# adaLN group 5 of a diffusion backbone's mLSTM layer: from TensorE's rows in the heads to VectorE during the projections

## The chip, the cores and the metric

The kernel runs on one core of one Trainium2 chip. The metric is the device time of one execution in microseconds; less is better. It has a median of 1303.7 us over three runs (1302.11 to 1309.29). All data are fp32.

## The reference, cut to what matters

One step of a backbone of four layers, on 128 context tokens and 256 latent tokens of width 1024. Every layer has a token mixer (pooling, mLSTM, latent attention, pooling) and then a mixture of 16 experts, 2 for each token. Ahead of both stands an RMS norm whose result is modulated by adaLN:

```
m = silu(cvec) @ w_ada[i] + b_ada[i]        # (1024) @ (1024, 6144): shift, scale, gate for mixer, then for experts
h = modulate(rmsnorm(x, norm_mix[i]), m0, m1);  x = x + m2 * mixer(h)
h = modulate(rmsnorm(x, norm_ffn[i]), m3, m4);  x = x + m5 * moe(h)
```

There are two conditioning vectors, one for context, one for latents. The mLSTM mixer of layer 1 computes

```
proj = h @ w_in                              # q, k: 4 heads x 128; v, o: 4 heads x 256; 16 gates
h_f, st_f = mlstm_chunkwise(q, k, v, g[0], g[1], init_f)     # forward scan
h_b, st_b = mlstm_chunkwise(flip of all, g[2], g[3], init_b) # backward scan
y = (sigmoid(o) * rmsnorm_per_head(h_f + flip(h_b)) * head_g) @ w_out
```

## The kernel before, in words

The six adaLN vectors of a layer are made in three groups of 2048 columns: group g belongs to layer g // 3, so groups 3, 4 and 5 are layer 1's. Group 5 holds the experts' scale and gate of layer 1, and groups 6 and 7 belong to layer 2. Each group needs 8 row blocks of `w_ada` (128 x 2048, 1 MB). There are two ways to make a group.

By TensorE: `ada(g, rows)` (L539) takes a block from the ring and runs four matmuls of 128x2 by 128x512 into four strips of PSUM bank 7. A matmul shows as two instructions, so a block is 8 and a group 64.

By VectorE: `mix(g, rows)` (L1644) multiplies a block by the conditioning value of each partition and adds it to an accumulator in SBUF, once for each of the two conditioning vectors (L1661; the first block is a plain product, L1664). The first block's part for accumulator 0 is made by ScalarE (`mixed_first`, L1295, L1300), and VectorE waits for it (`acc_set`). `ada_sum(g)` (L550) then sums both accumulators over the partitions by 8 matmuls (16 instructions).

Both ways go on alike: ScalarE copies bank 7 to `mrow` (`mod_rows`, L1288, L1293), TensorE turns it (`ada_columns`, L562, L566), VectorE adds the bias (`mod_columns`, L1624, L1629). Bank 7 and `mrow` hold one group at a time, so groups pass in order. Before, group 4 is mixed by VectorE and groups 5, 6 and 7 go by TensorE. The table `ACC` (L313) says where a group's accumulators lie, in pieces, since they live in space that is free at the time.

The ring (L53 to L56) has 12 slots of 1 MB for all weights. SP's queue loads the units in the order of the list `units`; unit u waits until unit u - 12 was used (L472).

TensorE's order in the mLSTM mixer (L701) is written out by hand: query and key projections (8 chunks), value projections (L729, 12 chunks of 128 tokens by 256 columns), the turns of the gate rows (L741), group 4's sum, gate projections (L750, 12 chunks), then the heads (L813). Projections use banks 5 and 6 in turn, and ScalarE copies each chunk out (L1358 for values, L1362 and L1364 for gates).

A head h makes its scores, the broadcast of running maxima (L782), two key products, and six numerators (L793), three for each direction, in three banks in turn. VectorE masks (L1775), weighs (L1787 to L1792), copies the two new states out of PSUM (L1805, L1806), divides (L1812 to L1820) and gates (L1827). ScalarE makes the exponentials (L1376, L1379), copies numerators (L1411), makes the carry's exponential (`carry_of`, L1386), the squares (L1420) and the output gate (L1429), and copies the turned head (L1394). VectorE's order for a head is: mask of head h+1, states of h, weights of h+1, division of direction 0, carry of h+1, division of direction 1, gating of h. The rows of groups 5, 6 and 7 stand between TensorE's instructions: for example four rows of group 5 while the first head's weights are made, two among the numerators of head 0, two behind the first numerator of head 1, and six of group 7 after the last head.

## Time and profile before

| What | Value |
|---|---|
| Median of three runs | 1303.7 us |
| The profiled execution's own time | 1300.99 us |
| Its span | 1299.3 us |
| Mean granted TensorE clock | 0.949 |
| TensorE busy | 1175.7 us, 90% |
| VectorE busy | 548.3 us, 42% |
| ScalarE busy | 328.3 us, 25% |
| Layer 1's value projections | from 316.2 us |
| Layer 1's gate projections | from 360.8 us |
| Heads | from 404.0 us |
| Output projection | from 478.2 us |

The span runs from the first to the last instruction of the profiled execution; its own time is what the run took as a whole. Busy times overlap between engines. A granted clock of 1.00 is 2.4 GHz, 0.50 is 1.2 GHz.

### The profile page before, as it was taken

Reading aid. Unit: us, or ns where it says so; the run is one execution under the profiler, and the core shown is the slowest. Engines: PE = TensorE matmul, PEld = TensorE weight load, DVE = VectorE, ACT = ScalarE, POOL = GpSimd, SP = SyncE. Lnnn points to the kernel's source line nnn. Section 1 sums busy time; section 2 is a strip of 40 time slices with the busy share of each in tenths; the row PEclk is TensorE's granted clock in tenths of the full one; section 3 lists DMA queues with packets and bytes.
Section 4 is the critical chain, followed back from the end, with each engine's and each line's share of the span. In section 5 each row is a group of like instructions: output and inputs, shape, how many; then the busy total and the mean of one; then the engine's idle time right before and its main releaser. Section 6 shows DMA issues by size and latency. Waiting matters only on the chain.

```text
span 1299.3 us, 24638 instructions
## 1 busy us (share of the span) xinstructions
PE 1175.7 (90%) x10246; PEld 702.6 (54%) x10246; DVE 548.3 (42%) x1318; ACT 328.3 (25%) x721; POOL 123.2 (9%) x188
## 2 busy tenths in 40 slices
PE   4788998889999989899987999999799997799986
PEld 2346554446886545655535844555564545564544
DVE  1355211259002549731117876459841115741113
ACT  1240111240123540411115411340411114411113
POOL 2000110210000000101120000000011120011111
PEclk9898998999999999899997999899799997799998
DMA  9999999799426789398979973106489987578983
GB/s 352 402 422 420 416 407 422 299 388 336 176 97 225 270 314 388 120 398 343 405 307 363 347 282 127 59 1 251 187 315 362 415 332 298 213 300 355 376 364 137
DMA packets 89708, 389.56 MB, mean 300 GB/s; under 512 B 10456, under 2 KB 38604, under 8 KB 53240
## 3 DMA queue, kind: packets, MB, share of 16 engines
q1 hardware_dynamic: 71568, 336.61, 65.7%
q0 software_dynamic: 17456, 51.07, 10.8%
q8 instruction: 85, 1.39, 0.4%
q10 hardware_dynamic: 568, 0.23, 0.1%
q14 instruction: 31, 0.25, 0.1%
HBM read 370.96 MB, written 27.96 MB: 307 GB/s over the span
## 4 chain that ended last, share of the span: by engine, by line
PE 75%; DMA 12%; DVE 5%; ACT 4%; issue 2%; POOL 1%; ACTq 0%; POOLq 0%; SPq 0%; DVEq 0%
PE bank L525 68%; DMA sb_ring<-in_w_ada 3%; PE bank L1068 3%; DMA sb_ring<-in_w_exp_down 2%; DMA slot_out<-sb_arena,sb_homes 2%; DMA sb_arena<-slot_out,sb_slots 2%; DMA token_rows<-sb_arena 1%; POOL sb_arena L2331 1%; DMA sb_arena<-in_b_ada 1%; PE bank L1086 1%; DVE sb_xT L2184 1%; DVE sb_hT L1671 1%; PE bank L1017 1%; DMA sb_arena<-token_rows,sb_rows 1%; ACT sb_hT L1340 1%
## 5 line engine op out<-in xcount | busy, mean ns | idle before, releaser
L525 PE MATMUL bank<-sb_ring,sb_arena 128*32 128x256 f32 (+1 forms) x6112 | 451.0, 429 | 19.3 <-DMA sb_ring<-in_w_exp_down 8.3
L525 PEld LDWEIGHTS bank<-sb_ring,sb_arena 128*32 128x32 f32 x6112 | 212.9, 111 | 199.2 <-issue 110.3
L525 PE MATMUL bank<-sb_ring,sb_hT 128*128 128x256 f32 x624 | 143.0, 392 | 4.1 <-ACT sb_hT L1330 4.1
L525 PE MATMUL bank<-sb_arena 128*128 128x128 f32 (+11 forms) x776 | 137.9, 355 | 8.7 <-ACT sb_arena L1497 2.3
L525 PEld LDWEIGHTS bank<-sb_ring,sb_hT 128*128 128x128 f32 x624 | 122.4, 197 | 25.5 <-issue 7.8
L2131 DVE TENSOR_TENSOR sb_arena<-sb_arena,bank 128x256 f32<-128x256 f32 x40 | 16.8, 421 | 251.8 <-PE bank L525 251.8
L525 PEld LDWEIGHTS bank<-sb_arena 128*128 128x128 f32 (+2 forms) x776 | 99.7, 188 | 42.1 <-issue 18.6
L1661 DVE SCALAR_TENSOR_TENSOR sb_arena<-sb_ring,sb_cond,sb_arena 128x2048 f32<-128x2048 f32 (+1 forms) x56 | 114.3, 2079 | 0.1
L525 PE MATMUL bank<-sb_arena,sb_ring 128*128 128x384 f32 (+2 forms) x288 | 93.9, 501 | 0.0
L525 PE MATMUL bank<-sb_hT,sb_ring 128*128 128x384 f32 x256 | 84.9, 494 | 2.6 <-ACT sb_hT L1330 2.6
L2138 DVE COPY sb_arena<-bank 128x512 f32<-128x512 f32 x40 | 27.7, 692 | 131.8 <-PE bank L525 131.8
L525 PEld LDWEIGHTS bank<-sb_arena,sb_ring 128*128 128x128 f32 (+1 forms) x288 | 49.1, 178 | 41.3 <-issue 15.9
L525 PEld LDWEIGHTS bank<-sb_hT,sb_ring 128*128 128x128 f32 x256 | 49.2, 193 | 37.5 <-issue 4.3
L1518 ACT ACTIVATE sb_arena<-bank 128x512 f32<-128x512 f32 x40 | 23.9, 597 | 158.8 <-PE bank L1068 141.1
L525 PE MATMUL bank<-sb_ring,sb_cond 128*2 128x512 f32 x448 | 55.6, 621 | 6.7 <-DMA sb_ring<-in_w_ada 6.4
L1310 ACT ACTIVATE sb_scratch<-sb_xT 128x768 f32<-128x768 f32 (+1 forms) x45 | 31.4, 713 | 108.8 <-DVE sb_xT L1688 98.9
L1522 ACT ACTIVATE sb_arena<-bank 128x256 f32<-128x256 f32 x40 | 15.4, 385 | 155.4 <-PE bank L525 155.4
L1671 DVE SCALAR_TENSOR_TENSOR sb_hT<-sb_xT,sb_amp,sb_rstd 128x128 f32<-128x128 f32 (+1 forms) x128 | 43.1, 411 | 15.4 <-ACT sb_rstd L1323 15.4
L2310 POOL DMA_INDIRECT slot_out<-sb_arena,sb_homes x27 | 27.1, 1004 | 223.1 <-DVE sb_arena L2138 219.9
L2299 POOL DMA_INDIRECT sb_arena<-token_rows,sb_rows x36 | 36.8, 1021 | 119.9 <-DVE sb_slots L2166 71.6
L1534 ACT ACTIVATE sb_arena<-bank 128x512 f32<-128x512 f32 x40 | 23.9, 597 | 82.5 <-PE bank L525 82.5
L2290 POOL DMA_DIRECT2D token_rows<-sb_arena x12 | 6.5, 540 | 389.0 <-ACT sb_arena L1497 388.9
(343 smaller groups left out, 1162.8 us busy)
## 6 DMA issues: line engine op xcount, KB each, us to landing
sb_ring<-in_w_ada SPq DMA_DIRECT2D x96, 1024.0 KB, 10.7
sb_ring<-in_w_exp_gate SPq DMA_DIRECT2D x60, 1024.0 KB, 10.1
sb_ring<-in_w_exp_up SPq DMA_DIRECT2D x60, 1024.0 KB, 12.7
sb_ring<-in_w_exp_down SPq DMA_DIRECT2D x60, 1024.0 KB, 15.0
sb_ring<-in_w_mlstm_in SPq DMA_DIRECT2D x12, 1024.0 KB, 9.4
token_rows<-sb_arena POOLq DMA_DIRECT2D x12, 512.0 KB, 4.2
slot_out<-sb_arena POOLq DMA_DIRECT2D x9, 512.0 KB, 8.9
sb_scratch<-in_w_exp_gate SPq DMA_DIRECT2D x4, 1024.0 KB, 7.1
```

Of the source, the lines that this page charges most:

```text
L525: return pe.matmul(out, lhsT, rhs, start=first, stop=last)
L1068: ins = pe.transpose(ps[2 + c][:, k * P:(k + 1) * P], xg[:, (o - 1) % 2, (4 * c + k) * P:(4 * c + k + 1) * P], ident[:, :])
L1310: act.activation(sq[:, a:b, :], xT[:, a:b, :], ACT.Square).then_inc(sq_ready, 1)
L1518: act.activation(xgT[:, o % 2, 0:4, :].rearrange("p k s -> p (k s)"), ps[2][:, :], ACT.Copy).then_inc(xa_ready, 1)
L1522: act.activation(sil[:, :], ps[0][:, 0:FE], ACT.Silu).then_inc(sil_ready, 1)
L1534: act.activation(ysb[:, o % 2, 0:512], ps[5][:, :], ACT.Copy).then_inc(ya_ready, 1)
L1661: ins = v.scalar_tensor_tensor(out=ap, in0=w[:, a:b], scalar=cond[:, k, c:c + 1], in1=ap, op0=ALU.mult, op1=ALU.add)
L1671: v.scalar_tensor_tensor(out=hT[:, k, a:b], in0=xT[:, k, a:b], scalar=gain[:, k, c:c + 1], in1=rstd[:, a:b], op0=ALU.mult, op1=ALU.mult).t ...
L2131: v.tensor_tensor(hid[:, :].rearrange("p (j q) -> p j q", j=2), sil[:, :].rearrange("p (q j) -> p j q", j=2), ps[1][:, 0:FE].rearrange("p ...
L2138: v.tensor_copy(ysb[:, o % 2, 512:1024], ps[6][:, :]).then_inc(yb_ready, 1)
L2299: g.indirect_dma_start(out=xg[:, (o - 1) % 2, :], out_offset=None, in_=Xg, in_offset=bass.IndirectOffsetOnAxis(ap=rows[:, o:o + 1], axis=0 ...
L2310: g.indirect_dma_start(out=Yg, out_offset=bass.IndirectOffsetOnAxis(ap=homes[:, o:o + 1], axis=0), in_=ysb[:, o % 2, :], in_offset=None, b ...
```

## The change: group 5 by VectorE, turns and group 4's sum earlier

Group 5 gets accumulators. Accumulator 0 lies in three pieces of 1024, 512 and 512 columns, accumulator 1 in one of 2048; they take the place of the gate rows (`grow`), which are last read by the turns and by two small DMAs (`out_m`), and of parts of `scratch` that the output gate of heads 2 and 3 is written to later. Its eight blocks are loaded between the value weights and behind the first gate weights. The turns move ahead of the value projections, group 4's sum behind value chunk 3 and its columns behind chunk 6. Group 5's sum comes behind gate chunk 2 and its columns behind chunk 5. In the heads the rows of groups 6 and 7 are placed anew, and `mod_rows` of group 6 moves from among head 1's numerators to behind them. Heads are computed in the order 0 to 3, as before.

```diff
+        in_gates = [[(view(8204, 1024), 0, 1024), (scratch[:, 512:1024], 1024, 1536), (scratch[:, 1536:2048], 1536, 2048)],
+                    [(view(6156, 2048), 0, 2048)]]
-        ACC = {4: in_squares, 8: in_values, 9: in_keys, 10: in_latents, 11: in_keys}
+        ACC = {4: in_squares, 5: in_gates, 8: in_values, 9: in_keys, 10: in_latents, 11: in_keys}
-        ADA_MIXER = [(), (5, 6, 7), (), ()]
+        ADA_MIXER = [(), (6, 7), (), ()]
...
# order of loads
                     if i == 0:
                         mixed_units(4, 6, 7)
+                    else:
+                        mixed_units(5, 2 * i - 2, 2 * i - 1)
                 for i in range(4):
                     add((w[:, 2048 + i * 256:2048 + (i + 1) * 256], KC, 256), 2048, (o_full, NT * (i + 1)))
+                    if i == 0:
+                        mixed_units(5, 6, 7)
...
# TensorE: the turns now stand ahead of the value projections; in these
-                ada_sum(4)
+                        if c == 3:
+                            ada_sum(4)
+                        if c == 6:
+                            ada_columns(4)
# and in the gate projections
-                        if c == 4:
-                            ada_columns(4)
+                        if c == 2:
+                            ada_sum(5)
+                        if c == 5:
+                            ada_columns(5)
# heads
-                ada(g4, 0, 1, 2, 3)
+                ada(near, 0, 1, 2, 3)
...
+                    if h == 2:
+                        ada_columns(near)
                     for c in range(2 * NT):
                         numerator(h, c // NT, c % NT)
-                        if h % 2 == 0 and c == (2 if h == 0 else 3):
-                            ada(g4 + h // 2, 4, 5)
-                        if h % 2 and c == 0:
-                            ada(g4 + h // 2, 6, 7)
-                        if h % 2 and c == 4:
-                            ada_columns(g4 + h // 2)
-                        if h % 2 and c == 5:
-                            ada(g5 + h // 2, 0, 1)
-                        if h == 2 and c == 0:
-                            ada(g5, 2, 3)
+                        if h == 1 and c == 2:
+                            ada(near, 6, 7)
+                        if h == 2 and c == 3:
+                            ada(far_group, 0, 1)
+                    if h == 0:
+                        ada(near, 4, 5)
+                    if h == 2:
+                        ada(far_group, 2, 3)
                     if h:
                         turn_head(h - 1)
-                ada(g6, 2, 3, 4, 5, 6, 7)
+                ada(far_group, 4, 5, 6, 7)
...
# ScalarE: value chunks, gate chunks, heads
+                    if c == 4:
+                        mod_rows(4)
+                        mixed_first(5)
-                    if c == 1:
-                        mod_rows(4)
+                    if c == 3:
+                        mod_rows(5)
-                        if h % 2 and c == NT - 1:
-                            mod_rows(ADA_MIXER[1][h // 2])
+                    if h == 1:
+                        mod_rows(ADA_MIXER[1][0])
                     if h + 1 < MH:
                         carry_of(h + 1)
...
# VectorE, after group 4 and the copy of the turned rows
+                v.wait_ge(out_m, 32)
+                mix(5, 0, 1, 2)
                 mod_columns(4)
+                mix(5, 3, 4, 5, 6, 7)
+                mod_columns(5)
```

Here `near` is group 6 and `far_group` group 7. VectorE adds group 6's bias in head 2.

## Rows read from the trace of the kernel before

**Rows 1.** The page: the chain that ended last, by engine.
```profile
PE 75%; DMA 12%; DVE 5%; ACT 4%; issue 2%; POOL 1%; ACTq 0%; POOLq 0%; SPq 0%; DVEq 0%
```
**Rows 2.** Stretches: length; PE, PEld, DVE, ACT, POOL busy (instructions); clock, DMA share, GB/s.
```profile
316.00:358.00 42.00, 42.00 (x198) 36.63 (x196) 8.87 (x6) 4.85 (x13) 0.00 (x0) 1.00 0.57 210
361.00:403.00 42.00, 41.95 (x196) 36.59 (x195) 0.19 (x1) 9.31 (x24) 0.00 (x0) 1.00 0.25 85
441.00:455.00 14.00, 14.00 (x82) 8.12 (x81) 7.12 (x23) 8.88 (x30) 1.07 (x2) 1.00 0.91 355
```
**Rows 3.** TensorE in order of time, projections: start, us, instructions, [idle before].
```profile
316.24 41.60 PE L525 MATMUL bank<-sb_ring,sb_hT 128*128 128x256 f32 x192
357.77 1.28 PE L746 MATMUL bank<-sb_ident,sb_arena 4*128 4x4 f32 x18
358.98 1.46 PE L525 MATMUL bank<-sb_scratch,sb_order 128*2 128x512 f32 x10
...
360.81 17.53 PE L525 MATMUL bank<-sb_ring,sb_hT 128*128 128x256 f32 x80
378.18 0.60 PE L566 MATMUL bank<-sb_ident,sb_mrow 128*128 128x128 f32 x4
378.62 24.34 PE L525 MATMUL bank<-sb_ring,sb_hT 128*128 128x256 f32 x112
403.99 1.38 PE L525 MATMUL bank<-sb_arena 128*128 128x128 f32 x10 [1.03 <-ACT sb_arena L1369]
```
**Rows 4.** VectorE in order of time: group 4, and head 3's last division.
```profile
302.71 1.28 DVE L1661 SCALAR_TENSOR_TENSOR sb_arena<-sb_ring,sb_cond,sb_arena 128x1024 f32<-128x1024 f32 x1
...
307.37 1.28 DVE L1661 SCALAR_TENSOR_TENSOR sb_arena<-sb_ring,sb_cond,sb_arena 128x1024 f32<-128x1024 f32 x1
...
322.53 2.35 DVE L1661 SCALAR_TENSOR_TENSOR sb_scratch<-sb_ring,sb_cond,sb_scratch 128x2048 f32<-128x2048 f32 x1
...
469.78 1.28 DVE L1820 SCALAR_TENSOR_TENSOR sb_arena<-sb_arena 128x256 f32<-128x256 f32 x3
```
**Rows 5.** ScalarE in order of time: first block, mrow, head 1's last numerator, squares.
```profile
282.70 1.99 ACT L1300 ACTIVATE sb_scratch<-sb_ring,sb_cond 128x2048 f32<-128x2048 f32 x1
...
368.76 0.58 ACT L1293 ACTIVATE sb_mrow<-bank 128x512 f32<-128x512 f32 x1
...
438.26 0.39 ACT L1411 ACTIVATE sb_arena<-bank 128x257 f32<-128x257 f32 x1 [0.92 <-PE bank L525]
...
471.93 0.41 ACT L1420 ACTIVATE sb_arena<-sb_arena 128x256 f32<-128x256 f32 x1
```
**Rows 6.** The chain that ended last: heads' last numerators and the return to TensorE.
```profile
422.58 0.39 ACT sb_arena L1411
...
431.07 5.85 PE bank L525 x18
...
453.93 0.39 ACT sb_arena L1411
```
**Rows 7.** TensorE in order of time, heads, columns as in rows 3.
```profile
417.84 1.90 PE L525 MATMUL bank<-sb_ring,sb_cond 128*2 128x512 f32 x16
...
431.07 0.70 PE L525 MATMUL bank<-sb_arena,sb_hT 128*128 128x257 f32 x2 [2.49 <-DVE sb_arena L1806]
...
461.49 0.70 PE L525 MATMUL bank<-sb_arena,sb_hT 128*128 128x257 f32 x2 [2.92 <-DVE sb_arena L1806]
...
476.58 0.82 PE L810 MATMUL bank<-sb_ident,sb_arena 128*128 128x128 f32 x6
478.22 0.95 PE L525 MATMUL bank<-sb_w_rt,sb_mod 128*1 128x16 f32 x32 [0.81 <-ACT sb_arena L1394]
```
**Rows 8.** Stretches of 2 us behind the gap at 431.07, columns as in rows 2.
```profile
431.00:433.00 2.00, 1.93 (x7) 1.65 (x8) 1.76 (x7) 2.00 (x8) 1.07 (x2) 0.77 0.98 414
433.00:435.00 2.00, 2.00 (x7) 1.54 (x6) 0.59 (x2) 0.31 (x2) 0.00 (x0) 0.50 0.98 397
435.00:437.00 2.00, 2.00 (x11) 1.70 (x10) 1.39 (x6) 1.08 (x4) 0.00 (x0) 0.87 0.06 25
```

More of the change, by code:

```diff
@@ L727, in mlstm @@
                         ins.then_inc(qk_full, 1)
+                pe.wait_ge(rows_done, 1)
+                for d in range(2):
+                    for q, src in enumerate((rA, rS, rE)):
+                        for t in range(NT):
+                            c = ((d * 3 + q) * NT + t) * MH
+                            ins = pe.transpose(ps[4][:, 64 + c:64 + c + MH], src[:, d, t * P:(t + 1) * P], ident[0:MH, 0:MH])
+                ins.then_inc(turns_full, 1)
                 for i in range(4):
@@ L739, in mlstm @@
                         ins.then_inc(v_full, 1)
-                pe.wait_ge(rows_done, 1)
-                for d in range(2):
-                    for q, src in enumerate((rA, rS, rE)):
-                        for t in range(NT):
-                            c = ((d * 3 + q) * NT + t) * MH
-                            ins = pe.transpose(ps[4][:, 64 + c:64 + c + MH], src[:, d, t * P:(t + 1) * P], ident[0:MH, 0:MH])
-                ins.then_inc(turns_full, 1)
-                ada_sum(4)
+                        if c == 3:
+                            ada_sum(4)
+                        if c == 6:
+                            ada_columns(4)
                 for i in range(4):
@@ L765, in mlstm @@
                 pe.wait_ge(l_ready, 12)
-                g4, g5, g6 = ADA_MIXER[1]
+                near, far_group = ADA_MIXER[1]
                 state["item"] = 0
@@ L845, in mlstm @@
                 project(r, lambda k: (qT if k % 2 == 0 else kT)[:, k // 2, :], hsT_ready, [8] * KC)
-                ada_columns(g6)
+                ada_columns(far_group)
             def mla(r):
@@ L1430, in mlstm @@
                 turned_head(MH - 1)
-                mod_rows(ADA_MIXER[1][2])
+                mod_rows(ADA_MIXER[1][1])
                 mixed_first(8)
@@ L1838, in mlstm @@
                     divided(h, 0)
-                    if h % 2:
-                        mod_columns(ADA_MIXER[1][h // 2])
+                    if h == 2:
+                        mod_columns(ADA_MIXER[1][0])
                     if h + 1 < MH:
@@ L2240, in _ @@
                 if kind == 1:
-                    mod_columns(ADA_MIXER[1][2])
+                    mod_columns(ADA_MIXER[1][1])
                 if L == 0:
```

## The prediction

> **What bounds the kernel now.** I read the page first. The chain that ended last is TensorE for 75% of the span [rows 1], so the question at each edit is whether it lies on TensorE's own line or beside it. Then a table of stretches over layer 1's mLSTM, then each engine's order of instructions there, and last the chain of waits through the four heads.
>
> The stage has two parts with different limits. In the value and gate projections (316 to 403 us) TensorE is busy without a break, VectorE works 8.9 us of the first 42 and 0.2 of the second 42 [rows 2]: TensorE bounds, and whatever it is given there lengthens the stage one for one. In the heads (404 to 478 us) it is mixed: TensorE is full from 441 to 455 [rows 2], but stands idle for 2.49 us before 431.07 and for 2.92 before 461.49, both times for VectorE's copy of a state, L1806 [rows 7]. The chain says why [rows 6]: from the evacuation of a head's last numerator (422.58) it runs in the code's order through ScalarE's carry (L1386), VectorE's division (L1820), ScalarE's squares and exponential (L1420, L1429), VectorE's mask (L1775) and state copy, and only at 431.07 back to TensorE: 8.5 us in which TensorE has nothing of its own but turns, scores, keys and the next head's first numerator. The adaLN rows stand in that gap as filling. For the last pair (453.93 to 461.49) it is 7.56 us [rows 6, 7], since no mask follows.
>
> **The change part by part.** Times are those of the profiled execution before; "heads frame" means that the shift of the projections is added at the end.
>
> *Turns and group 4's sum.* They took 357.77 to 358.98 and 358.98 to 360.81 between the projections [rows 3], 1.21 and 1.83 us on TensorE. Now they stand before the first and after the fourth value chunk. Both are moved along a line without gaps: 0. What they wait for is there: VectorE's last row of group 4 ends at 322.53 + 2.35 = 324.9 [rows 4], the sum comes at 316.24 + 1.21 + 4 x 3.46 = 331.3 (a chunk is 41.5/12 = 3.46, from 316.24 to 357.77). Value projections then end at 317.45 + 41.5 + 1.83 + 0.44 (group 4's columns, 378.18 to 378.62) = 361.2.
>
> *Group 5 on VectorE.* A row of group 4 costs 307.37 - 302.71 = 4.66 us, from one operation of 2048 and two of 1024 [rows 4]. That gives 1.04 ns a column and 0.13 us an operation. Group 5 has 2048, 1024 and twice 512: 2.26 + 1.20 + 2 x 0.66 = 4.78 us. VectorE begins at 325.1 (after copying rowc), does row 0's half (a plain product; 1.3 by estimate, 2.35 at most, without effect on what follows) and row 1's half (2.3), and stops at 328.7: its other half starts from what ScalarE sets (acc_set). ScalarE gets there after value chunk 4 (ends 336.6; copy 0.4), mod_rows(4) (0.58) and three pieces of the 2048 that took 1.99 [rows 5]: 339.8. This wait is free for VectorE, which has nothing else; behind ScalarE's 2.7 us stands only the copy of chunk 5 (full at 340.0). Then row 1's rest 2.5, row 2 4.8, mod_columns(4) 0.35 (its columns are turned at 343.9), rows 3 to 7 23.9: **371.4**.
>
> *Group 5's sum and columns.* They come after the third and sixth gate chunk. Chunk 2 ends at 361.2 + 3 x 3.46 = **371.6**, so TensorE arrives 0.2 us after VectorE is done. Gate chunks 3 to 11 and all heads queue behind this wait. The sum costs 1.83 and the columns 0.44, both on a line without gaps. The lower bound of the wait is 0; the upper takes the full durations 2.35 + 1.28 + 2 x 0.75 a row, 5.1, so 0.35 more over nearly 7 rows: 2.4 late, 2.2 us of wait. I take 0, since group 4's spacing was measured in the same loop. Gate projections end at 371.6 + 1.83 + 9 x 3.46 + 0.44 = 404.9, against 402.7 before: **+2.2 us**, 1.83 of it the sum and 0.44 the columns that leave the heads.
>
> The Trainium skill, VectorE: DVE Perf Modes, section "The TRN2 errata — SBUF-src ops pay a fixed extra latency per instruction", speaks against cutting an operand into pieces: each instruction pays a fixed cost, and it gives (N+151)/0.96 ns for an fp32 operation of two tensors, 0.69 us at 512 and 2.29 at 2048. The rows agree that there is such a part, but the spacing shows it smaller. An estimate from the page's formula is 4.89 us a row; VectorE would end some 0.8 us later, and the sum would be 0.6 us longer.
>
> *Loads.* On SP's queue group 5's eight rows move ahead of v2, v3 and the gate weights, to where rows of group 4 free slots. Queue and bytes stay the same, nothing is issued twice. The last value and first gate weights then wait for slots that come free with the last key chunk (316) and the third value chunk (328), in a stretch where DMA is 25% to 57% busy [rows 2]; they are wanted from 350 and 361 on. The latest, o2 and o3, wait for group 5's row 1 (342) and are wanted after 382: 0. Below zero is excluded, as TensorE waits for no load here.
>
> *The heads.* 64 instructions leave; 16 of this form (128x512, two rows as at 417.84 [rows 7]) take 1.83 us start to start, as the sum of group 4 does [rows 3]: 7.3 us of TensorE, and one set of columns. What is that worth? I follow the order head by head.
> Head 0: its two rows stood between numerators 2 and 3, on the chain. They now follow the last numerator, in the gap: -1.83. The return to TensorE for head 1 is at 431.07 - 1.83 = 429.24; TensorE is empty from 426.7, 2.5 us, as long as before (2.49).
> Head 1: two rows of group 6 go from the gap in front to the numerators, behind number 2: +1.83; the columns are gone: -0.44. Last numerator evacuated at 437.8, before 438.26 [rows 5]. But mod_rows(6) now stands between this evacuation and the carry, 0.55 us of ScalarE on the chain: +0.55. The return for head 2 is then 437.8 + 0.55 + 8.4 = 446.8, what it was (446.83). In front of it TensorE had four rows, 3.7 us, that are gone: it is empty from 442.8, 4.0 us, where it had no gap.
> Head 2: same numerators, same two rows among them. After the gaps of 2.49 and 2.92 us [rows 7] the granted clock was 0.50 for 0.92 + 2.00 + 0.52 = 3.4 us (0.77, 0.50 and 0.87 in three stretches of 2 us [rows 8]), which on a full TensorE costs half of it, 1.7 us. A gap of 4.0 should do the same here: **+1.7**. The lower bound is 0, the upper two such stretches, 3.4.
> Head 3: return at 455.6 + 7.56 = 463.2, before 461.49; the clock falls as before. Without columns (-0.44) the last evacuation is 1.2 late, at 469.9. Turning head 2 no longer waits for two rows, so ScalarE's squares, which began at 471.93 though VectorE had divided by 469.78 + 1.28 = 471.06 [rows 4, 5], are not pushed back by it: -0.87. Four last rows instead of six end at 474.2, and the last turn waits for the gated head at 476.0, where it used to wait for the rows until 476.58 [rows 7]. The output projection starts at 477.65 instead of 478.22: **-0.6 us**.
> So of 7.7 us taken out only 0.6 arrive (2.3 but for the clock). What is late next is the ScalarE and VectorE chain, not TensorE.
> Two short gaps in front of the output projection (1.8 and 0.8 us, before 0.8) may bring one more half-clock stretch, 0 to 1.7; I take 0, as the gap of 1.03 at 403.99 [rows 3] brought none.
>
> *Later.* Loads of the output weights come earlier, since rows of group 6 free slots sooner; TensorE waits for none of them now, so 0. From the output projection on the order is the same, group 7's columns still follow the projection, and routing and experts start from it: the shift is carried through.
>
> **Sum:** +2.2 - 0.6 = +1.6 us. The profiled execution took 1300.99 us (span 1299.3), so it would take 1302.6; the median of the runs is 2.7 us above it, so 1305.3. Range of this case alone: 1302 to 1309.
>
> **Rivals.**
> (a) TensorE bounds the heads after all. For it: 90% busy over the span, and no idle from 441 to 455 [rows 2]. Against it: three idle stretches on the chain. Then the whole 7.3 + 0.44 comes off: +2.2 - 7.7 = -5.5, 1298.2.
> (b) The gap before head 2 doesn't lower the clock, or the one before head 1 no longer does. For it: the clock is full in all of 441 to 455 today. Against: both gaps over 2.4 us were followed by it. +1.6 - 1.7 = 0, 1303.6; with both -1.8.
> (c) TensorE waits at group 5's sum, because VectorE's rows take their full durations or ScalarE's part comes late; the shift to VectorE then isn't a hidden one. Decides when a row exceeds 4.8 us. +1.6 + 2.2 = +3.8, 1307.5.
> (d) The other side, slower by over 0.5%: TensorE's clock. The filling was what kept the gaps short. If each of the three gaps between heads brings two stretches at half clock and the output projection starts in one, it is 3 x 1.7 + 1.7 = 6.8 on top, +8.4, 1312.1. Place: numerators behind each gap. It decides once a gap is followed by more than one stretch of 3.4 us; the 2.49 and 2.92 were not.
>
> **How the numbers follow.** About 0.5% (6.5 us) is what a measurement of this kernel can tell from no change; its three runs spread over 7 us. Forecast 0.52, (a) 0.14, (b) 0.16, (c) 0.10, (d) 0.08. The range 1298.5 to 1311 takes in (b), (c), nearly all of (a), and leaves (d) and stray runs out. Faster by over 0.5%: a part of (a) with the spread, 0.08. Slower: (d) and the upper spread of (c) and the forecast, 0.13. Same: 0.79.
>
> **What would show it.** Right: TensorE without a gap in both projections, the gate projections ending 2.2 us later after the turns; VectorE's last group 5 operation within 1 us of gate chunk 2; the heads' stretch within 1.5 us of 74.2; a new gap of about 4 us before head 2's second numerator with clock 0.50 behind it; group 6's mrow copy just ahead of the carry. Wrong: heads shorter by over 4 us (then (a)), a TensorE wait on VectorE L1661 over 1 us (then (c)), or a difference that lies outside 316 to 521 us, which would mean that a load or the clock elsewhere decides.

## The result, and the profile after

The changed kernel takes 1307.11 us (median of 18 runs, 1302.97 to 1315.81) beside 1302.51 us for the kernel before on the same chip: a ratio of 1.0046, 95% interval 1.0026 to 1.0065. Run a second time beside other kernels (e11 below) it had 1.0084 (1.0051 to 1.0118). So it is slower, by 0.3 to 1.2%, where the forecast was +1.6 us, 0.12%. The measured 1307.11 lies in the range that was given (1298.5 to 1311) and the sign is that of the sum, but the sum was too small: +4.6 us in the medians, +6.2 between the two profiled executions (1307.2 and 1300.99). That the time still lies in the range is due to the range, which is 12.5 us wide, and not to the sum.

The profiled execution after has a span of 1305.2 us and a mean granted clock of 0.946. In its code the lines stand a little lower: L525 is now L531 (TensorE's products), L1661 is L1675 (VectorE's mixing), L1806 is L1824 (state copy), L1411 is L1425, L1386 is L1400, L1293 is L1304. In the experiments they are off by a few lines more or less; L1822, L1826, L1808 and L1804 are all the state copy.

TensorE's order of time in the projections, after (columns as in [rows 3]):

```profile
318.07 1.28 PE L740 MATMUL bank<-sb_ident,sb_arena 4*128 4x4 f32 x18
319.28 14.08 PE L531 MATMUL bank<-sb_ring,sb_hT 128*128 128x256 f32 x64
333.29 1.46 PE L531 MATMUL bank<-sb_scratch,sb_order 128*2 128x512 f32 x10
...
346.02 27.79 PE L531 MATMUL bank<-sb_ring,sb_hT 128*128 128x256 f32 x128
373.74 0.60 PE L531 MATMUL bank<-sb_arena,sb_order 128*2 128x512 f32 x2
...
375.57 10.63 PE L531 MATMUL bank<-sb_ring,sb_hT 128*128 128x256 f32 x48
...
408.39 1.38 PE L531 MATMUL bank<-sb_arena 128*128 128x128 f32 x10 [1.03 <-ACT sb_arena L1383]
```

There is no idle time from the turns (318.07) to the end of the gate projections; the stretch to the first scores is 90.32 us, and was 316.24 to 403.99, 87.75 us [rows 3]. Group 5's sum starts at 373.74 without a wait. VectorE was done just in time:

```profile
342.03 1.28 DVE L1675 SCALAR_TENSOR_TENSOR sb_arena<-sb_ring,sb_cond,sb_arena 128x1024 f32<-128x1024 f32 x1 [11.64 <-ACT sb_scratch L1311]
343.23 1.41 DVE L1675 SCALAR_TENSOR_TENSOR sb_scratch<-sb_ring,sb_cond,sb_scratch 128x512 f32<-128x512 f32 x2
...
367.38 1.41 DVE L1675 SCALAR_TENSOR_TENSOR sb_scratch<-sb_ring,sb_cond,sb_scratch 128x512 f32<-128x512 f32 x2
368.70 3.54 DVE L1675 SCALAR_TENSOR_TENSOR sb_arena<-sb_ring,sb_cond,sb_arena 128x2048 f32<-128x2048 f32 x2
372.16 1.41 DVE L1675 SCALAR_TENSOR_TENSOR sb_scratch<-sb_ring,sb_cond,sb_scratch 128x512 f32<-128x512 f32 x2
```

A row takes 372.16 - 367.38 = 4.78 us, and the last one ends at 373.57, 0.17 us ahead of the sum. VectorE's 11.64 us wait for ScalarE (342.03) cost TensorE nothing.

The heads are where the forecast and the trace part. TensorE's order of time after (columns as in [rows 7]):

```profile
411.53 5.02 PE L531 MATMUL bank<-sb_ring,sb_cond 128*2 128x512 f32 x32
...
421.37 0.70 PE L531 MATMUL bank<-sb_arena,sb_hT 128*128 128x257 f32 x2 [0.41 <-DVE sb_arena L1824]
...
434.92 1.22 PE L531 MATMUL bank<-sb_arena,sb_hT 128*128 128x257 f32 x2 [2.29 <-DVE sb_arena L1824]
...
452.65 1.22 PE L531 MATMUL bank<-sb_arena,sb_hT 128*128 128x257 f32 x2 [3.64 <-DVE sb_arena L1824]
...
459.57 1.90 PE L531 MATMUL bank<-sb_ring,sb_cond 128*2 128x512 f32 x16 [1.42 <-issue]
...
471.44 0.70 PE L531 MATMUL bank<-sb_arena,sb_hT 128*128 128x257 f32 x2 [3.45 <-DVE sb_arena L1824]
...
484.33 0.88 PE L821 MATMUL bank<-sb_ident,sb_arena 128*128 128x128 f32 x6 [1.77 <-DVE sb_arena L1845]
486.02 1.01 PE L531 MATMUL bank<-sb_w_rt,sb_mod 128*1 128x16 f32 x32 [0.81 <-ACT sb_arena L1408]
```

And four lines of the kernel before that the table below needs beside those of [rows 7]:

```profile
406.89 3.62 PE L525 MATMUL bank<-sb_ring,sb_cond 128*2 128x512 f32 x32
...
415.48 0.70 PE L525 MATMUL bank<-sb_arena,sb_hT 128*128 128x257 f32 x2 [0.42 <-DVE sb_arena L1806]
...
446.83 0.70 PE L525 MATMUL bank<-sb_arena,sb_hT 128*128 128x257 f32 x2
...
449.62 1.90 PE L525 MATMUL bank<-sb_ring,sb_cond 128*2 128x512 f32 x16
```

The number in brackets is TensorE's idle time and who ended it. Before there were two gaps over 2 us [rows 7]; now there are three (2.29, 3.64, 3.45), a new one of 1.42 among head 2's numerators, and 1.77 behind the last head. The heads take 77.63 us instead of 74.23. A head's "return" is the moment when TensorE goes on behind the head's first numerator, with the state that VectorE copied (415.48, 431.07, 446.83 and 461.49 before). From one return to the next:

| Stretch | Before | After | Difference | Forecast |
|---|---|---|---|---|
| Turns or value projections to first scores | 87.75 | 90.32 | +2.6 | +2.2 |
| First scores to return in head 0 | 11.49 | 12.98 | +1.5 | 0 |
| to return in head 1 | 15.59 | 13.55 | -2.0 | -1.8 |
| to return in head 2 | 15.76 | 17.73 | +2.0 | +1.8 |
| to return in head 3 | 14.66 | 18.79 | +4.1 | +1.7 |
| to the output projection | 16.73 | 14.58 | -2.2 | -2.3 |
| Output projection, to group 7's columns | 42.26 | 43.57 | +1.3 | 0 |

That is +7.3 us for the whole, of which the forecast had +1.6. Outside these stretches, where the order of instructions is the same, the two executions differ by +1.8 us ahead of 316 us and by -3.2 behind the output projection. Both are differences of single executions: the start of the first row of the table lies anywhere from 314.7 to 318.1 us in the thirteen profiles of this document (316.75 in the changed kernel's second one), and behind the output projection the clock was at 1.2 GHz for 94.5 us before and 87.6 us after, which is worth 3.4 us where TensorE is busy. The medians say +4.6.

The granted clock in stretches of 2 us, behind the gaps at 452.65 and 486.02 (columns as in [rows 2]; the clock is the third number from the right):

```profile
451.00:453.00 2.00, 0.35 (x1) 0.35 (x2) 1.99 (x7) 1.23 (x5) 0.11 (x1) 0.74 0.00 0
453.00:455.00 2.00, 2.00 (x6) 1.54 (x6) 1.77 (x5) 1.64 (x7) 0.96 (x2) 0.50 0.37 131
455.00:457.00 2.00, 2.00 (x6) 1.63 (x5) 0.18 (x1) 0.15 (x1) 0.00 (x0) 0.50 0.00 0
457.00:459.00 2.00, 1.15 (x3) 0.34 (x1) 1.14 (x6) 0.77 (x2) 0.00 (x0) 0.55 0.00 0
...
487.00:489.00 2.00, 2.00 (x5) 1.13 (x4) 1.78 (x4) 1.35 (x1) 0.00 (x0) 0.50 0.99 406
```

Around the gap of 3.64 us the clock is at 1.2 GHz for 1.04 + 2 + 2 + 1.8 = 6.8 us, twice as long as behind the 2.49 before [rows 8]. It begins at 451.96, 0.7 us before TensorE returns, and ends in the wait at 458.8, so some of it falls on idle time and costs nothing.

The wait that the forecast did not have is seen on VectorE, after:

```profile
457.75 0.16 DVE L1830 SCALAR_TENSOR_TENSOR sb_arena<-sb_arena 128x3 f32<-128x3 f32 x1 [2.57 <-ACT sb_arena L1425]
...
458.36 0.88 DVE L1836 TENSOR_SCALAR sb_arena<-sb_arena 128x256 f32<-128x256 f32 x3
459.28 0.19 DVE L1643 TENSOR_TENSOR sb_mod<-bank,sb_b_ada 128x32 f32<-128x32 f32 x1
```

L1643 is `mod_columns(6)`. It was moved to head 2 behind the division of direction 0, and this division starts only when numerator 2 of head 2 is copied. TensorE's first row of group 7 (`ada(7, 0)`, behind numerator 3 of head 2) needs bank 7 free, and so waits for it: it ends at 459.28 + 0.19 = 459.47 on VectorE, and the row starts at 459.57 on TensorE. The same 0.10 us lie between the two in e2 (453.91 and 454.01) and e11 (459.62 and 459.72). Numerators 4 and 5 and head 3's keys stand behind it.

And ScalarE, after, with `mod_rows(6)` on the chain between the last numerator's copy and the carry:

```profile
443.67 0.39 ACT L1425 ACTIVATE sb_arena<-bank 128x257 f32<-128x257 f32 x1 [0.48 <-PE bank L531]
443.95 0.59 ACT L1304 ACTIVATE sb_mrow<-bank 128x512 f32<-128x512 f32 x1
444.43 0.84 ACT L1400 ACTIVATE sb_arena<-bank,sb_m_all 128x256 f32<-128x256 f32 x2
```

### The profile page after: what moved, and what is told of

Its sections match the earlier page's. It is cut to its first block, busy times and chain, and to the rows that moved or that the text cites. A ratio compares the mean times of both kernels' runs of the same rounds, so it can differ in the third digit from the quotient of the medians.

```text
span 1305.2 us, 24581 instructions
## 1 busy us (share of the span) xinstructions
PE 1178.1 (90%) x10198; PEld 716.1 (55%) x10198; DVE 582.3 (45%) x1347; ACT 330.6 (25%) x724; POOL 123.2 (9%) x188
## 4 chain that ended last, share of the span: by engine, by line
PE 74%; DMA 11%; DVE 6%; ACT 4%; issue 3%; POOL 1%; SPq 1%; ACTq 0%; POOLq 0%; DVEq 0%
PE bank L531 68%; DMA sb_ring<-in_w_ada 3%; PE bank L1079 3%; DMA slot_out<-sb_arena,sb_homes 2%; DMA sb_ring<-in_w_exp_down 2%; DMA sb_arena<-slot_out,sb_slots 2%; POOL sb_arena L2349 1%; DMA sb_arena<-in_b_ada 1%; DVE sb_xT L2202 1%; PE bank L1097 1%; DVE sb_hT L1685 1%; PE bank L1028 1%; DMA sb_arena<-token_rows,sb_rows 1%; DMA slot_out<-sb_arena 1%; ACT sb_hT L1351 1%
## 5 line engine op out<-in xcount | busy, mean ns | idle before, releaser
L531 PE MATMUL bank<-sb_ring,sb_arena 128*32 128x256 f32 (+1 forms) x6112 | 456.9, 430 | 21.7 <-DMA sb_ring<-in_w_exp_down 9.7
L531 PEld LDWEIGHTS bank<-sb_ring,sb_arena 128*32 128x32 f32 x6112 | 228.0, 111 | 192.3 <-issue 114.1
L531 PE MATMUL bank<-sb_arena 128*128 128x128 f32 (+11 forms) x776 | 140.1, 359 | 8.2 <-ACT sb_arena L1511 2.3
L1675 DVE SCALAR_TENSOR_TENSOR sb_arena<-sb_ring,sb_cond,sb_arena 128x2048 f32<-128x2048 f32 (+1 forms) x70 | 139.2, 2025 | 11.9 <-ACT sb_scratch L1311 11.6
L531 PE MATMUL bank<-sb_ring,sb_hT 128*128 128x256 f32 x624 | 140.6, 387 | 4.2 <-ACT sb_hT L1341 4.2
L531 PEld LDWEIGHTS bank<-sb_ring,sb_hT 128*128 128x128 f32 x624 | 119.9, 194 | 25.0 <-issue 8.2
L531 PEld LDWEIGHTS bank<-sb_arena 128*128 128x128 f32 (+2 forms) x776 | 100.8, 190 | 42.4 <-issue 20.1
L531 PE MATMUL bank<-sb_arena,sb_ring 128*128 128x384 f32 (+2 forms) x288 | 95.2, 506 | 0.0
L531 PE MATMUL bank<-sb_hT,sb_ring 128*128 128x384 f32 x256 | 87.1, 503 | 2.6 <-ACT sb_hT L1341 2.6
L531 PEld LDWEIGHTS bank<-sb_arena,sb_ring 128*128 128x128 f32 (+1 forms) x288 | 49.7, 180 | 42.0 <-issue 17.0
L531 PEld LDWEIGHTS bank<-sb_hT,sb_ring 128*128 128x128 f32 x256 | 50.5, 198 | 38.7 <-issue 6.0
L531 PE MATMUL bank<-sb_ring,sb_cond 128*2 128x512 f32 x384 | 50.2, 650 | 8.9 <-DMA sb_ring<-in_w_ada 7.2
```

Of the source, the lines that this page charges most:

```text
L531: return pe.matmul(out, lhsT, rhs, start=first, stop=last)
L1675: ins = v.scalar_tensor_tensor(out=ap, in0=w[:, a:b], scalar=cond[:, k, c:c + 1], in1=ap, op0=ALU.mult, op1=ALU.add)
```

## The experiments

Theory after the result: the heads are bound by a chain through ScalarE and VectorE, so rows taken from TensorE there earn nothing unless they stood on the chain; they leave gaps, and gaps bring TensorE's half clock; and the new places put one wait on the chain. Rivals: TensorE bounds the heads; the half-clock stretches come by chance; the moves in the projections are what costs.

All ratios are to the kernel before on the same chip, from 6 to 18 runs of each kernel and 18 to 35 of the kernel before. The stretches are of each kernel's one profiled execution, and that of the kernel before is from the first chip only.

| Kernel | Ratio (95%) | Projections | Heads | Mean clock in heads | Output projection |
|---|---|---|---|---|---|
| before | 1 | 87.75 | 74.23 | 0.95 | 42.26 |
| changed | 1.0046 (1.0026, 1.0065) | 90.32 | 77.63 | 0.89 | 43.57 |
| changed again (e11) | 1.0084 (1.0051, 1.0118) | 90.32 | 80.36 | 0.85 | 43.71 |
| e1 rows behind head 2 | 1.0005 (0.9981, 1.0029) | 90.32 | 77.36 | 0.85 | 43.75 |
| e2 changed, gaps filled | 0.9993 (0.9966, 1.0021) | 90.32 | 73.81 | 0.95 | 43.66 |
| e3 rows in the gaps | 0.9965 (0.9941, 0.9990) | 90.32 | 68.33 | 0.92 | 44.84 |
| e4 moves only | 1.0022 (0.9993, 1.0051) | 87.86 | 75.92 | 0.93 | 42.27 |
| e5 e3 filled | 0.9982 (0.9957, 1.0008) | 90.32 | 71.07 | 0.98 | 42.27 |
| e6 old places | 1.0005 (0.9979, 1.0032) | 90.32 | 74.02 | 0.88 | 42.26 |
| e7 before, gaps filled | 0.9961 (0.9929, 0.9993) | 87.76 | 72.50 | 0.98 | 42.27 |
| e8 two rows last | 0.9972 (0.9944, 1.0000) | 90.32 | 71.31 | 0.88 | 43.46 |
| e9 all by TensorE, in gaps | 0.9957 (0.9927, 0.9987) | 87.75 | 68.24 | 0.97 | 42.26 |
| e10 e5, sized | 0.9971 (0.9940, 1.0003) | 90.32 | 67.88 | 0.95 | 42.27 |

### e1: without the wait in head 2

```diff
-                        if h == 2 and c == 3:
-                            ada(far_group, 0, 1)
                     if h == 2:
-                        ada(far_group, 2, 3)
+                        ada(far_group, 0, 1, 2, 3)
```

> The changed kernel, with group 7's first two rows moved from behind numerator 3 of head 2 to behind its last numerator. Theory (wait): ada(7, 0) waits for VectorE's mod_columns(6), which stands behind VectorE's division of head 2, and TensorE's idle 1.42 us ahead of these rows lies on the chain. Then head 2's stretch (18.8 us between returns) shrinks by 1.4 for the wait and 1.8 for the rows, 3.2 in all, and the idle gap in front of head 3 shrinks from 3.45 to 1.6 us: the kernel is 3 us faster than the changed one, +1.5 to +3 us against the one before. Rival (TensorE bounds): the rows cost the same wherever they stand, so only the 1.4 us can come off. Rival (half clock): the second 3.4 us stretch of half clock in head 2 came from the wait; it goes too, 1.7 us more.

The wait is gone (no idle time but the returns), and the stretch from head 2's return to head 3's is 453.89 to 469.85, 15.96 us instead of 18.79: -2.8 where 3.2 were expected, and 1.8 of the 2.8 are the two rows' own time, which left the chain with the wait. The gap did not shrink to 1.6, though:

```profile
460.67 3.61 PE L531 MATMUL bank<-sb_ring,sb_cond 128*2 128x512 f32 x32
464.21 0.87 PE L821 MATMUL bank<-sb_ident,sb_arena 128*128 128x128 f32 x6
...
469.85 0.70 PE L531 MATMUL bank<-sb_arena,sb_hT 128*128 128x257 f32 x2 [3.25 <-DVE sb_arena L1822]
```

ScalarE in the same execution says why:

```profile
464.80 1.05 ACT L1406 ACTIVATE sb_arena<-bank,sb_vecs 128x384 f32<-128x384 f32 x2 [2.91 <-PE bank L821]
465.74 0.41 ACT L1432 ACTIVATE sb_arena<-sb_arena 128x256 f32<-128x256 f32 x1
```

ScalarE copies the turned head 1 (L1406) ahead of head 2's squares (L1432), and the turn (L821) now stands behind four rows. It comes at 464.21, and the squares start only at 465.74. In the changed kernel the last numerator's copy and the squares are 467.31 - 463.87 = 3.4 us apart, here 465.74 - 460.78 = 5.0. So four rows ahead of a turn were too many here. The whole heads took 77.36 us, with more half clock (mean 0.85). The ratio is below the changed kernel's 1.0046, but their intervals touch.

### e2: work added in the gaps

```diff
+                    for _ in range((0, 5, 8, 8)[h] if d == 0 and t == 0 else 0):
+                        mm(b, a[:, d, t * P:(t + 1) * P], vx[:, t, h, :], True, True)
                     ins = mm(b, a[:, d, t * P:(t + 1) * P], vx[:, t, h, :], True, t == 0)
```

> The changed kernel, with work added: the first product of the first numerator is repeated 5 times in head 1 and 8 times in heads 2 and 3 (same operands, same bank, result overwritten by the same), 21 x 0.43 = 9 us of TensorE, put where it is idle for 2.3, 3.6 and 3.45 us. Theory (clock): the half-clock stretches behind these gaps are caused by them. Filled gaps bring no stretch: -1.7 us for head 1, -1.7 to -3.4 for head 2, -1.7 for head 3, so 4 to 6 us faster than the changed kernel although it does more. Rival (the stretches come by chance or from something else): no faster, 0 to 1 us slower. Rival (TensorE bounds the heads): 9 us slower.

With 9 us of useless products TensorE is full across the gaps, and the heads take 73.81 us instead of 77.63, at a mean clock of 0.95 instead of 0.89. Only two idle times are left between head 0 and the last turn:

```profile
449.31 0.70 PE L531 MATMUL bank<-sb_arena,sb_hT 128*128 128x257 f32 x2 [0.20 <-DVE sb_arena L1826]
...
454.01 1.90 PE L531 MATMUL bank<-sb_ring,sb_cond 128*2 128x512 f32 x16 [1.84 <-issue]
```

The second is the wait for `mod_columns(6)` again, by itself: here, with the clock full around it, it is 1.84 us. From the return to this first row of group 7 it takes 454.01 - 449.31 = 4.70 us here, 449.62 - 446.83 = 2.79 in the kernel before and 459.57 - 452.65 = 6.92 in the changed one. So the wait is worth 1.9 us, and the half clock of the changed kernel the other 2.2. The ratio, 0.9993 (0.9966 to 1.0021), lies clear of the changed kernel's 1.0046 (1.0026 to 1.0065). "TensorE bounds the heads" would have made them 9 us longer and falls with this run. "By chance" is weakened, as three stretches went at once; e7 and e11 add to that.

### e3: the rows of groups 6 and 7 in the gaps

The calls that place these rows and columns in the changed kernel are taken out (not printed), and these put in:

```diff
                     for c in range(2 * NT):
                         numerator(h, c // NT, c % NT)
+                        if h == 1 and c == 0:
+                            ada(near, 6, 7)
+                        if h == 1 and c == 4:
+                            ada_columns(near)
+                        if h > 1 and c == 0:
+                            ada(far_group, 4 * h - 6, 4 * h - 5)
...
                     if h == 0:
                         ada(near, 4, 5)
+                    if h == 1:
+                        ada(far_group, 0, 1)
+                    if h == 2:
+                        ada(far_group, 4, 5)
```

with `mod_rows(6)` after head 1's numerator 2 and `mod_columns(6)` in head 1.

> The changed kernel with the rows of groups 6 and 7 placed in the gaps between heads and none among numerators: 4, 5 of group 6 behind head 0 and 6, 7 behind the first numerator of head 1; 0, 1 of group 7 behind head 1, 2, 3 behind head 2's first numerator, 4, 5 behind head 2, 6, 7 behind head 3's first numerator; none behind head 3. Group 6's copy to mrow stands after head 1's numerator 2, its columns after numerator 4. Theory (ScalarE and VectorE chain plus gaps): against the changed kernel -1.8 and -0.55 in head 1, -1.4 and -1.8 in head 2, and 2 to 4 half-clock stretches of 1.7 us less: 8 to 11 us faster than the changed one, so 3 to 6 us faster than the one before. Rival (TensorE bounds): the same rows at other places, at most 1.4 us faster than the changed one.

The heads take 68.33 us, 9.3 less than in the changed kernel with the same 16 blocks of rows, and the kernel is faster than the one before (0.9965). The rows cost nothing that shows in the gaps. What is left is the gap behind the last head:

```profile
474.08 1.54 PE L821 MATMUL bank<-sb_ident,sb_arena 128*128 128x128 f32 x6 [5.41 <-DVE sb_arena L1846]
476.30 1.01 PE L531 MATMUL bank<-sb_w_rt,sb_mod 128*1 128x16 f32 x32 [0.67 <-ACT sb_arena L1409]
```

The six turns take 1.54 us instead of 0.8 and the output projection 44.84 instead of 42.26: the half clock begins within the 5.41 idle us and lasts 10.2.

### e4: the moves in the value projections alone

The kernel before, with turns and group 4's sum and columns at their new places, and group 5 by TensorE as before.

> The kernel before with one part of the change alone: turns ahead of the value projections, group 4's sum behind value chunk 3, its columns behind chunk 6; group 5 stays with TensorE in the heads. Theory: 0 (within 1 us), as these are moves along a TensorE without gaps. Rival: the moves themselves cost the extra 2.6 us that the projections show, or ScalarE's copy to mrow among value chunks holds up TensorE; then 2 to 3 us slower.

Projections 87.86 us beside 87.75: the moves cost 0.1 us, and the 2.5 us up to 90.32 come with group 5's sum and columns (1.83 and 0.44). The ratio 1.0022 (0.9993 to 1.0051) doesn't tell it from no change. Its heads have the order of before and took 75.92, with one half-clock stretch more (clock 0.93), so 1.7 us of difference between two profiles can be the clock alone.

### e5 and e10: the last gaps filled with nothing

The edit is on top of e3's.

```diff
+                    for _ in range((0, 1, 0, 3)[h] if d == 0 and t == 0 else 0):
+                        mm(b, a[:, d, t * P:(t + 1) * P], vx[:, t, h, :], True, True)
...
                 pe.transpose(ps[2][0:8, 0:P], nout, ident[:, :]).then_inc(turns_full, 1)
+                for _ in range(16):          # 7 in e10
+                    mm(ps[3][:, 0:TOK], ident[:, :], xT[:, 0, :], True, True)
```

> The kernel with rows in the gaps (e3), plus work that computes nothing new: the first product of the first numerator repeated once in head 1 and three times in head 3, and 16 products of 128x128 by 128x384 into a free PSUM bank behind the last head's columns of n. They fill the idle 0.47, 1.63 and 5.41 us that e3 still has. Theory (clock): e3's 10.2 us at half clock from 472.3 on, behind its gap of 5.41 us, cost some 4 to 5 us of turns and output projection; filled, they go: 3 to 5 us faster than e3, 1293 to 1295 us beside 1301 for the kernel before. Rival (stretches come from something else): same as e3, or up to 0.5 us slower.

> As e5, with 7 products behind the last head instead of 16. In e5 they took 10.3 us, twice what was meant, and the last head's turn stood 4.9 us late behind them; the clock had no stretch there. Theory (chain): heads 66 to 67 us beside 71.1, output projection at full clock, 4 to 5 us faster than e5, so 7 to 8 faster than before. Rival: the 7 leave a gap that brings a half-clock stretch, 2 to 3 us faster than e5 only.

e5 was a miss in its size: 16 products are 32 instructions of 0.32 us, and the last turn stood behind them until 475.00:

```profile
464.68 10.49 PE L531 MATMUL bank<-sb_xT,sb_ident 128*128 128x384 f32 x32
475.00 0.82 PE L823 MATMUL bank<-sb_ident,sb_arena 128*128 128x128 f32 x6
```

In e10, with 14 instructions, the gap ahead of that turn is short:

```profile
467.10 4.68 PE L531 MATMUL bank<-sb_xT,sb_ident 128*128 128x384 f32 x14
472.68 0.87 PE L823 MATMUL bank<-sb_ident,sb_arena 128*128 128x128 f32 x6 [0.90 <-DVE sb_arena L1850]
```

In both the output projection runs at full clock, 42.27 us, where e3 had 44.84. Heads are 71.07 and 67.88 us. In the profiles the half clock behaves as expected. The medians fall short of what was expected: e5 is not faster than e3, and e10 is 4.1 us faster than the kernel before (1292.84 and 1296.92), not 7 to 8. 0.9982 and 0.9971 are not told apart from each other or from e3.

### e6: group 5's rows gone, the others at their old places

> The changed kernel, but in the heads groups 6 and 7 stand where they stood before: group 5's rows and columns are simply gone (none while the first weights are made, none in head 0, none behind head 1's first numerator). It separates the removal from the new places. Theory: -1.8 us (head 0's two rows) and -0.4 (columns), all else bound by the ScalarE and VectorE chain, so the heads take 72 us but for the clock; the emptied gaps (3.7 us at the start, 4.4 in front of head 1's second numerator, 2.9 in front of head 3's) each bring a half-clock stretch or two. Heads 72 to 76 us, beside 77.6 in the changed kernel, as neither the 1.4 us wait nor the rows among head 1's numerators are there: 0 to 4 us slower than before, 2 to 5 faster than the changed one. Rival (TensorE bounds): -7.7 us in the heads, 5 us faster than before.

Its edit is `before`'s order of heads without the calls for group 5. TensorE is idle 3.42 us at the start, 4.32 in front of head 1's second numerator, 2.93 in head 3. Heads 74.02 us at a mean clock of 0.88, ratio 1.0005 (0.9979 to 1.0032). Taking 7.7 us from TensorE leaves the heads as they were: 0.2 us shorter, with more half clock. At nearly the same mean clock (0.88 and 0.89) the new places of the changed kernel took 3.6 us more than the old ones; they have the wait in head 2 and two rows and mrow's copy ahead of head 1's carry. In the ratios the two just overlap (up to 1.0032 here, from 1.0026 there).

### e7: the kernel before with its two gaps filled

The edit of e2 on the kernel before, with (0, 5, 0, 6).

> The kernel before, unchanged but for work that computes nothing new: the first product of the first numerator repeated 5 times in head 1 and 6 times in head 3, 4.8 us of TensorE in its two idle gaps of 2.49 and 2.92 us. Theory (clock): both stretches at half clock behind the gaps go, 1.7 us each: 2 to 3.4 us faster than before, heads 70.8 to 72 us instead of 74.2. Rival: no effect or slower by up to 0.5 us.

0.9961 (0.9929 to 0.9993): 4.8 us of useless work make the kernel before faster. Both stretches at half clock behind the returns are gone; one is left elsewhere, in head 0 from 416.5 us on (heads 72.50 us, mean clock 0.98). The two returns:

```profile
432.88 0.70 PE L525 MATMUL bank<-sb_arena,sb_hT 128*128 128x257 f32 x2 [0.33 <-DVE sb_arena L1808]
...
461.63 0.70 PE L525 MATMUL bank<-sb_arena,sb_hT 128*128 128x257 f32 x2 [0.33 <-DVE sb_arena L1808]
```

And its clock (third number from the right) in head 0 and from there to the last heads:

```profile
416.00:418.00 2.00, 2.00 (x7) 1.60 (x6) 1.85 (x5) 1.61 (x6) 0.98 (x2) 0.63 1.00 422
...
420.00:474.00 54.00, 52.90 (x330) 31.22 (x326) 28.10 (x96) 30.61 (x95) 3.21 (x6) 1.00 0.76 280
```

### e8: two of e3's rows behind the last head

`ada(far_group, 6, 7)` stands after the loop instead of behind head 3's first numerator.

> The kernel with rows in the gaps (e3), with the last two rows of group 7 behind the last head instead of in the gap in front of head 3's second numerator. Both places are idle anyhow: e3 had gaps of 1.63 and 5.41 us, this one has 3.46 and 3.6. Theory (chain): no row of these lies on the chain, so only the clock changes: the long stretch behind the last head shrinks (10.2 to 3.4 us, -3.4) and one in front of head 3 comes (+1.7): 0 to 3 us faster than e3. Rival (rows cost wherever they are): same as e3.

Gaps 3.46 and 3.49 us instead of 1.63 and 5.41. The output projection gained 1.4 us (43.46) and the heads lost 3.0 (71.31, mean clock 0.88). Ratio 0.9972 (0.9944 to 1.0000), not told apart from e3, where 0 to 3 us less were expected. Two gaps of 3.5 us were no better than one of 1.6 and one of 5.4.

### e9: all rows by TensorE, placed in the gaps

```diff
-                        if h % 2 == 0 and c == (2 if h == 0 else 3):
-                            ada(g4 + h // 2, 4, 5)
...
-                        if h % 2 and c == 5:
-                            ada(g5 + h // 2, 0, 1)
...
+                    if h < 3:
+                        ada(g4 + (h + 1) // 2, *((4, 5), (0, 1), (4, 5))[h])
                     if h:
                         turn_head(h - 1)
-                ada(g6, 2, 3, 4, 5, 6, 7)
+                ada(g6, *range(KC))
```

on the kernel before.

> The kernel before (group 5 by TensorE, nothing mixed by VectorE in the projections), with the 24 rows of the heads placed in the gaps: 4 at the start as before, 4 in each of the three gaps between heads (two behind a head's last numerator, two behind the next head's first), the 8 of group 7 behind the last head, none among numerators. Theory (chain and gaps): -1.8 in head 0 and -1.8 in head 2, and its two gaps of 2.49 and 2.92 us shrink to about 0.5 and 1, so the half-clock stretches behind them go (-1.7 each); the 8 last rows end no later than 6 did behind two others. Heads 67 to 69 us beside 74.2, projections 87.8 beside the 90.3 of the kernels that mix group 5 by VectorE: 5 to 7 us faster than before. Rival (TensorE bounds the heads, its rows have to be taken out to gain): 0.

Heads 68.24 us, with 24 blocks of rows in them:

```profile
431.77 0.70 PE L525 MATMUL bank<-sb_arena,sb_hT 128*128 128x257 f32 x2 [0.47 <-DVE sb_arena L1804]
...
458.49 0.70 PE L525 MATMUL bank<-sb_arena,sb_hT 128*128 128x257 f32 x2 [1.63 <-DVE sb_arena L1804]
...
464.55 7.05 PE L525 MATMUL bank<-sb_ring,sb_cond 128*2 128x512 f32 x64
...
471.63 0.82 PE L810 MATMUL bank<-sb_ident,sb_arena 128*128 128x128 f32 x6
473.27 0.95 PE L525 MATMUL bank<-sb_w_rt,sb_mod 128*1 128x16 f32 x32 [0.81 <-ACT sb_arena L1392]
```

1290.19 us beside 1296.92 for the kernel before and 1306.50 for the changed one on that chip; 0.9957 (0.9927 to 0.9987). It beats both kernels, and doesn't need VectorE's mixing of group 5, so it saves the 2.6 us of the projections too (87.75 and 90.32). From e3 and e10, which keep that mixing, its ratio is not told apart.

### e11: the changed kernel again

> The changed kernel itself, to stand beside the other two on one chip and to see which of its half-clock stretches come back. Theory (clock by gaps): the heads take 76 to 79 us again, and the stretches behind the gaps in front of heads 1, 2 and 3 and in front of the output projection return at the same places (26.8, 43.9, 64.3 and 78.0 us after the heads' start); 1.003 to 1.006 of the kernel before. Rival (chance): they lie elsewhere.

The gaps come back to 0.01 us (2.30, 3.64, 3.45, 1.78), the half clock at each of them too, and once more ahead of head 0 and at the output projection (43.71 us). The wait in head 2 is 1.84 us here and was 1.42. How long a stretch is differs: the mean clock in the heads is 0.85 here and 0.89 there, and the heads take 80.36 and 77.63 us. That is more than the 76 to 79 us expected, and so is the ratio. So the places go with the gaps, and the length is that execution's own.

## Why the prediction was right or wrong

*Turns and group 4's sum, 0.* Right: 0.1 us (e4).

*Group 5 on VectorE, done at 371.4, TensorE there at 371.6.* Right. A row takes 4.78 us as worked out, and the sum starts 0.17 us after the last operation, without a wait; rival (c) did not happen. With the 1.83 us by which this execution's stage began later taken off, both came 0.3 us later than worked out (371.7 and 371.9), so the margin held, but by little. Two operations of 512 take 1.41 us and one of 1024 takes 1.28, so there is a fixed part in each. The Trainium skill (VectorE: DVE Perf Modes, "The TRN2 errata") states such a fixed cost of each instruction. An estimate from that page's formula was 4.89 us a row, 0.11 more than measured. In the trace the next operation starts before the last one's record ends (368.70 against 367.38 + 1.41 = 368.79).

*The projections, +2.2.* +2.6; the 1.83 and 0.44 were right, and some 0.3 us lie in the places around the inserted instructions, 0.1 of it in the moves alone (e4).

*Loads, 0.* Right: TensorE waits for no load in these stretches.

*Head 0, -1.8, and head 1, +1.8 (two rows among the numerators, mrow's copy on the chain).* Right: -2.0 and +2.0, gaps of 2.29 and 3.64 where 2.5 and 4.0 were given.

*Head 2, +1.7, "same numerators, same two rows among them".* This step failed. It measured +4.1. The two rows at numerator 3 are at the same place, but they are another group's: before, they were rows 4 and 5 of group 6, now they are rows 0 and 1 of group 7, and row 0 waits for the bias of the group before. I had followed `mod_columns(6)` on VectorE only as a cost to VectorE and not asked who waits for it. It was put at nothing and was worth 1.9 us, as e2 shows with the clock full around it (in the changed kernel it stands as 1.42 us of idle time, since TensorE came there late). In e1 it is gone, and the stretch falls by 2.8, the two rows' own 1.8 among them. All of the +4.1 lies ahead of this row: from it to the return in head 3 both kernels take 11.87 us. The rest of the 4.1, 2.2 us, is half clock, 6.8 us of it instead of the 3.4 that I took from the shorter gaps before; it was given 1.7, and the upper bound of 3.4 us for the clock held.

*First scores to head 0, 0, and the output projection, 0.* Both were undersized: +1.5 and +1.3 us of half clock. For the second I had given 0 to 1.7 and taken 0 after the gap of 1.03; the pair of 1.77 and 0.81 us did bring one, in each of the four profiles with that pair (43.57, 43.75, 43.66 and 43.71 us). For the first I had no term. In all twelve other profiles a half-clock stretch begins 2.2 to 12.4 us after the first scores; only the one execution from which I worked had none, which was luck of that profile. Where it begins goes with the kernel. In the four profiles with group 5 by TensorE (before, e4, e7, e9) the stretch to the return in head 0 takes 11.49 us each time, and in the three of them that have half clock it comes only behind this stretch (e4: 17.28 us to the return in head 1 instead of 15.59). In eight of the nine with group 5 by VectorE, all but e5, half clock begins 2.2 to 3.0 us after the first scores, and the stretch takes 12.85 to 14.68 us. So the 1.5 us do go with the change, and not with its moves alone (e4). No run shows what in it brings them, with an idle time of 1.03 us ahead of the first scores in every profile; that is open.

*Last head, -2.3.* Right: -2.2.

*"Of 7.7 us taken out only 0.6 arrive."* The mechanism was right, and stronger than stated: by e6 it is 0.2 at the old places, and at the new places they cost 3.4. Rival (a), TensorE bounds the heads, is refuted by e2, e6 and e9. Rival (d), the clock, was given 0.08 and is the larger part of the 5.7 us that were missing: three extra stretches came (head 2's second, 0.5 us over the 1.7; the start, 1.5; the output projection, 1.3), 3.3 us in all, not the 6.8 it was priced at, beside 1.9 for the wait. Its condition, more than one stretch of 3.4 us behind a gap, was met at one gap of three, and at two in e11; its "over 0.5%" was 0.46% in the first measurement and 0.84% in e11. I had underrated it because I took the two gaps of before as the scale for a gap half as long again. Of the signs that were named for being right, the heads "within 1.5 us of 74.2" failed: they took 77.63.

## What to carry to other kernels

Where a loop is bound by a chain through other engines, as these heads are, work of TensorE in its gaps costs nothing as long as it fits in them (e3; in e5 it did not), and it keeps the clock up. Taking 7.7 us of it out earned 0.2 us (e6), and the gaps it left came with more half clock. Move such work between the end of one turn of the chain and its return, and not among the instructions that feed it: 24 blocks of rows so placed (e9) took less time than 16 placed otherwise. When a filler is moved, ask what its first instruction waits for at the new place, and what stands behind it in other engines' orders (four rows ahead of the head's turn held up ScalarE's squares by 1.6 us).

## What the runs showed of the hardware

From the return in head 1 to the last head's turn, every gap of TensorE of 2.3 to 2.9 us but one (e6, 2.93 us) came with its half clock, for 3.4 to 6.8 us, and so did every gap of 3.25 to 5.41 us, for 3.4 to 10.2 us. The clock fell between 3.1 us before TensorE's return (within the gap) and 1.4 us after it. At gaps of 0.2 to 1.6 us between heads it never fell; but it did fall near the start of the heads in twelve of thirteen profiles, with idle times of 1.03 and 0.42 us there (in e6 3.42 besides), and behind the pair of 1.77 and 0.81 us ahead of the output projection in four of four. Filling the gaps with useless products made the kernel before faster (e7: 0.9961, with 4.8 us of work added) and shortened the changed kernel's heads by 3.8 us (e2). Two executions of the changed kernel, with the gaps between heads equal to 0.01 us, took 77.63 and 80.36 us for the heads; what differs is the length of their half-clock stretches (mean clock 0.89 and 0.85).
